# Level order, an earlier turn of K and half-array transposes in the RWKV recurrence of a two-block kernel

## The reference, cut to what matters

```python
def _rwkv7_step(S, inp):
    r, w, k, v, kk, a = inp
    sa = jnp.einsum('dbhij,dbhj->dbhi', S, -kk)
    S = S * w[..., None, :] + sa[..., None] * (kk * a)[..., None, :] + v[..., None] * k[..., None, :]
    y = jnp.einsum('dbhij,dbhj->dbhi', S, r)
    return S, y
```

## Time and profile before

| | us |
|---|---|
| median of three runs | 2919.23 |
| the profiled execution's own time | 2922.75 |
| its span | 2921.0 |
| TensorE busy in the span | 2863.0 |
| VectorE busy in the span | 1467.3 |
| ScalarE busy in the span | 1085.4 |

### The profile page before, as it was taken

The page is one execution under the profiler, slowest core; times in us unless marked ns, Lnnn a source line. Parts: engine busy times, 40 slices in busy tenths (PEclk is TensorE's granted clock), DMA queues, the critical chain, the costliest instruction groups (busy, mean ns, idle before and its releaser), DMA issues.

```text
span 2921.0 us, 43018 instructions
## 1 busy us (share of the span) xinstructions
PE 2863.0 (98%) x19334; PEld 2365.6 (81%) x19334; DVE 1467.3 (50%) x1431; ACT 1085.4 (37%) x1176; POOL 174.8 (6%) x94
## 2 busy tenths in 40 slices
PE   9999999999999999999999999999998998999998
PEld 7787788888889888888888888788877886888886
DVE  6766553443454544343454344555666555544432
ACT  5554532222454732222342223442244432332222
POOL 1002110000100010000110000330000000100001
PEclk9999999999999999999999999999999999999999
DMA  4220022323222022223222233321240003222222
GB/s 148 73 76 2 30 87 101 101 90 119 101 90 87 30 87 88 100 101 108 101 98 90 101 103 112 112 80 65 87 133 4 3 5 133 87 101 101 98 98 79
DMA packets 44887, 249.06 MB, mean 85 GB/s; under 512 B 8443, under 2 KB 12283, under 8 KB 17184
## 3 DMA queue, kind: packets, MB, share of 16 engines
q1 hardware_dynamic: 43552, 242.11, 24.2%
q10 hardware_dynamic: 1152, 4.19, 0.4%
HBM read 237.90 MB, written 8.39 MB: 84 GB/s over the span
## 4 chain that ended last, share of the span: by engine, by line
PE 91%; DVE 5%; ACT 3%; issue 1%; DMA 0%; POOL 0%; SPq 0%; DVEq 0%; ACTq 0%
PE ps L667 75%; PE ps L2909 6%; PE ps L1522 1%; PE ps L2493 1%; PE ps L2203 1%; PE ps L3961 1%; PE ps L2477 1%; PE ps L3944 1%; PE ps L3973 1%; PE ps L2174 0%; PE ps L3083 0%; DVE wlo L274 0%; DVE gdn_conv L1147 0%; ACT whi L268 0%; PE ps L426 0%
## 5 line engine op out<-in xcount | busy, mean ns | idle before, releaser
L274 DVE TENSOR_TENSOR wlo<-wraw,whi 128x2048 fp32r<-128x2048 f32 x210 | 486.5, 2317 | 911.0 <-ACT whi L268 906.9
L268 ACT ACTIVATE whi<-wraw 128x2048 fp32r<-128x2048 f32 x210 | 402.1, 1915 | 900.1 <-PE ps L667 900.1
L667 PE MATMUL ps<-ffn_xh,whi 128*128 128x512 f32 x1408 | 549.2, 390 | 0.2 <-DVE wlo L274 0.2
L667 PE MATMUL ps<-ffn_xh,wlo 128*128 128x512 f32 x1408 | 547.8, 389 | 0.0
L667 PE MATMUL ps<-ffn_xl,whi 128*128 128x512 f32 x1408 | 547.8, 389 | 0.0
L667 PEld LDWEIGHTS ps<-ffn_xh,whi 128*128 128x128 f32 x1408 | 264.3, 188 | 57.0 <-DVE wlo L274 1.0
L667 PEld LDWEIGHTS ps<-ffn_xl,whi 128*128 128x128 f32 x1408 | 264.3, 188 | 55.6 <-issue 0.7
L667 PEld LDWEIGHTS ps<-ffn_xh,wlo 128*128 128x128 f32 x1408 | 264.3, 188 | 54.7
L667 PE MATMUL ps<-ffn_uh,whi 128*128 128x512 f32 x704 | 274.1, 389 | 0.0
L667 PE MATMUL ps<-ffn_uh,wlo 128*128 128x512 f32 x704 | 273.9, 389 | 0.0
L667 PE MATMUL ps<-ffn_ul,whi 128*128 128x512 f32 x704 | 273.9, 389 | 0.0
(11 more groups left out here) (518 smaller groups left out, 4485.9 us busy)
## 6 DMA issues: line engine op xcount, KB each, us to landing
wraw<-in_weights SPq DMA_DIRECT2D x211, 1024.0 KB, 4.9
gates_kept<-gates_tmp ACTq DMA_DIRECT2D x8, 512.0 KB, 4.1
mix_gate<-gates_kept SPq DMA_DIRECT2D x8, 512.0 KB, 11.2
h<-in_x SPq DMA_DIRECT2D x4, 512.0 KB, 8.3
mix_y<-hz_kept SPq DMA_DIRECT2D x2, 1024.0 KB, 6.4
out<-out SPq DMA_DIRECT2D x4, 512.0 KB, 3.1
wraw<-in_weights SPq DMA_DIRECT2D x2, 512.0 KB, 6.7
ple_raw<-in_p SPq DMA_DIRECT2D x4, 256.0 KB, 5.2
```

The source lines that it names most:

```text
L268: c.nc.scalar.activation(c.whi[:, j % 2, :], c.wraw[:, j % 2, :], ACT.Copy).then_inc(c.hi_ready, 1)
L274: c.nc.vector.tensor_tensor(c.wlo[:, j % 2, :], c.wraw[:, j % 2, :], c.whi[:, j % 2, :].bitcast(F32), ALU.subtract).then_inc(c.lo_ready, 1)
L667: last = nc.tensor.matmul(pair[:, m, :], a, b, start=opens and n == 0 and wa + xa == 0, stop=closes and n == len(ks) - 1 and wa == 1)
```

## The change

Three edits. The level order becomes L L R R at every level: slots 7 to 25 hold L00 L01 R00 R01 L10 L11 R10 R11 and so on up to L40 L41 R40, then slot 26 the turn of `K`, slot 27 R41, slot 28 the turn of `B`. The turn of `K` goes to `A_BANK` and `C_BANK`, so it waits for the last `y` of the pair that steps, and the first z of the next steps waits for `Kt`. `pe_strict` now waits for the last `XT` of the build before, and the products with `Bt` wait for `Bt`. Third, in every turn the head on partitions 0 to 63 is turned by a transpose instruction in place of a matmul; the other head stays a matmul.

```diff
+    def turned(self, out, src):
+        nc, ident, (one, two) = self.c.nc, self.c.ident, self.halves()
+        nc.tensor.transpose(out(one), src(one), ident[one, one])
+        return nc.tensor.matmul(out(two), src(two), ident[two, two], start=True, stop=True)
...
         if part == 0:
+            if n == 0:
+                pe.wait_ge(*self.at("Kt", p))
             pe.wait_ge(*self.at("ST", 8 * p + n))
...
-                if n == 0:
-                    pe.wait_ge(*self.at("Kt", p))
...
             if n < NCH - 1:
+                if n == 0:
+                    pe.wait_ge(*self.at("Bt", p))
...
-        elif s in (7, 8):
-            self.pe_left(pe, k, 0, s - 7)
-        elif s == 9:
-            self.pe_right(pe, k, 0, 0)
-        elif 10 <= s < 26:
-            l, what = 1 + (s - 10) // 4, (s - 10) % 4
-            if what in (0, 2):
-                self.pe_left(pe, k, l, what // 2)
+        elif 7 <= s < 26:
+            l, what = divmod(s - 7, 4)
+            if what < 2:
+                self.pe_left(pe, k, l, what)
             else:
-                self.pe_right(pe, k, l - 1 if what == 1 else l, int(what == 1))
+                self.pe_right(pe, k, l, what - 2)
         elif s == 26:
+            pe.wait_ge(*(self.at("y", 8 * k - 1) if k else self.shift.free(len(RW_ORDER) - 1)))
+            self.pe_turn(pe, self.K[k % 2], (self.A_BANK, self.C_BANK), "tK")
+        elif s == 27:
             self.pe_right(pe, k, LEVELS - 1, 1)
-        elif s == 27:
-            self.pe_turn(pe, k, self.B, self.Z_BANK, "tB")
         elif s == 28:
-            self.pe_turn(pe, k, self.K, self.F_BANK, "tK")
+            pe.wait_ge(*self.at("XT", 10 * k + 2 * (LEVELS - 1)))
+            self.pe_turn(pe, self.B[k % 2], self.Z_BANK, "tB")
...
         elif k:
-            pe.wait_ge(*self.at("Kt", k - 1))
+            pe.wait_ge(*self.at("XT", 10 * k - 1))
```

More of the change, by code:

```diff
@@ L2750, in __init__ @@
         self.sems = {}
-        for engine, cycles in (("pe", ("kk", "lora", "vt", "BA", "KA", "MV", "Y", "Z", "tB tK", "z", "U", "dS",
+        for engine, cycles in (("pe", ("kk", "lora", "vt", "BA", "KA", "MV", "Y", "Z", "tK tB", "z", "U", "dS",
                                        "bonus turn g")),
                                ("act", ("u12", "kk2 log rs", "se sl s", "eB eR fac", "t3", "vtc", "XTe", "LT", "MVc", "ysc", "Yc",
[1 row of a table removed]
[1 row of a table added]
                                ("dve", ("neg", "eye", "floor nkk", "scan b kdir B K R A", "kd bonus1",
@@ L2845, in sync @@
             self.load_pair(sp, p, self.gl, self.gl_loaded, 2)
-        sp.wait_ge(*self.at("tK", HP - 1))
+        sp.wait_ge(*self.at("tB", HP - 1))
         sp.wait_ge(*self.at("dS", 8 * HP - 9))
@@ L3051, in pe_right, with pe_turn @@
         last.then_inc(*self.done("Z"))
-    def pe_turn(self, pe, k, what, banks, name):
-        src = what[k % 2]
-        pe.wait_ge(*self.at("XT", 10 * k + 2 * (LEVELS - 1) + (banks is self.F_BANK)))
+    def pe_turn(self, pe, src, banks, name):
         for d in range(2):
             for n in range(NCH):
-                last = self.both(lambda r: self.bank(banks[d])[r, n, :], lambda r: src[r, d, n, :],
-                                 lambda r: self.c.ident[r, r])
+                last = self.turned(lambda r: self.bank(banks[d])[r, n, :], lambda r: src[r, d, n, :])
         last.then_inc(*self.done(name))
@@ L3088, in pe_prepare @@
             for n in range(NCH):
-                last = self.both(lambda r: out[r, n, :], lambda r: u[r, 2 * HP + p, n * C7:(n + 1) * C7],
-                                 lambda r: self.c.ident[r, r])
+                last = self.turned(lambda r: out[r, n, :], lambda r: u[r, 2 * HP + p, n * C7:(n + 1) * C7])
             last.then_inc(*self.done("vt"))
@@ L3102, in pe_finish @@
             for n in range(NCH):
-                last = self.both(lambda r: out[r, n, :], lambda r: self.yp[r, n, :], lambda r: self.c.ident[r, r])
+                last = self.turned(lambda r: out[r, n, :], lambda r: self.yp[r, n, :])
             last.then_inc(*self.done("turn"))
@@ L3166, in act_build @@
                     .then_inc(*self.done("ysc"))
[L3167 to L3172, removed]
+        if 7 <= s < 26 and (s - 7) % 4 < 2:
+            self.act_left(act, k, *divmod(s - 7, 4))
+        elif s in (26, 28):
+            name, dst, banks = (("tK", self.Kt, (self.A_BANK, self.C_BANK)), ("tB", self.Bt, self.Z_BANK))[(s - 26) // 2]
             act.wait_ge(*self.at(name, k))
@@ L3347, in dve_build @@
                 .then_inc(*self.done("ys"))
[L3348 to L3353, removed]
+        if 7 <= s < 26 and (s - 7) % 4 >= 2:
+            l, what = divmod(s - 7, 4)
+            self.dve_right(dve, k, l, what - 2)
+        elif s == 27:
             self.dve_right(dve, k, LEVELS - 1, 1)
@@ L3410, in dve_prepare @@
             if p >= 2:
-                dve.wait_ge(*self.at("tK", p - 2))
+                dve.wait_ge(*self.at("tB", p - 2))
             eB = self.eB[:, :, 1 - d:1 - d + C7]
```

## The result

The changed kernel takes 3011.66 us (median of four runs, 3010.88 to 3014.51), the kernel before 2919.27 (2918.84 to 2923.47): the ratio is 1.0315 [1.0297, 1.0333], 3.2% slower, where 2912.3 was forecast and 2920.5 was the end of the range. The profiled execution took 3011.53 us, its span 3009.7.

A forecast was written before the change was run, and what follows sets the result against it. TensorE, busy for 98% of the span, was taken as the bound, so only its lost time in the recurrence could be won: 3.4 (level order) + 3.5 (early `K`) + 0 (transposes) = 6.9 us less, 2912.3; range 2905 to 2920.5.

The forecast's parts named there:

- One head by transposes: In the turns' 192 chunks: quarters keep their own pace, so 0; bounds 5.6 us won, 11.2 lost.
- Rival 4: In the 192 chunks: a transpose holds the array for itself, up to 58 ns each, 2923.5 us; chance 0.14.
- The clock: In the recurrence: pauses of like sum remain, so no change; bounds 4.3 us won, 5.1 lost.
- K turned early: Before the next build's first product: the wait for `Kt` goes, 1.15 us in three periods, 3.5 us less.
- Level order: In the recurrence's levels: TensorE's waits for `X` go, partly replaced by waits for `ST` and `Zs`; 3.4 us less.
- Rival 1: In the recurrence: VectorE and ScalarE take the level order's whole gain, only `Kt` waits go, 2915.7 us; chance 0.20.
- Rival 2: In the turns: issue is the bound, so transposes win 5.6 us more, 2906.7 us; chance 0.12.
- Rival 3: In period 1: the clock's fall goes with the pauses ahead of it, 4.3 us more won, 2908.0; chance 0.18.

The follow-up runs named there:

- e1: The changed kernel with both heads turned by plain matmuls again, level order and early turn of `K` kept: 2914.21 us, ratio 0.9981.
- e9: e1 with the first head's product in the large turns a plain matmul 128 columns wide, no transposes: 3022.96 us, ratio 1.0355.
- e3: The kernel before with the early turn of `K` alone, old level order and plain turns: 2916.61 us, ratio 0.9993.
- e4: The changed kernel with all transposes of a turn first, then all its matmuls: 2931.99 us, ratio 1.0043.
- e2: The kernel before with the level order L L R R alone, `K` turned last, plain turns: 2918.20 us, ratio 0.9997.
- e8: e1 with VectorE's preparation of the next pair one slot later, and period 0's late taps and `ST` reset moved: 2906.76 us, ratio 0.9958.
- e5: The changed kernel with transposes and matmuls of a turn alternating in groups of four chunks: 2954.80 us, ratio 1.0121.

## Why the prediction was wrong, by its steps

- **One head by transposes: this step failed.** It was priced at nothing, "each quarter has its own pace", with 11.2 us as the upper bound. The runs show 59 us in the turns at full clock, and, through the clock, about 40 more (21 in the turns, 15 to 19 outside); e1 puts the whole at 97. Two things were wrong in it. First, show four transposes in a row and one quarter alone, never a transpose between quarters, and their pace was taken for the pace of the mixture. The first of those four stands 149 ns behind the quarter's last record, so the price was in these rows too, at their edge. Second, the bound only counted the transposes' own 58 ns; a bound has to hold the cost of going from one kind of instruction to the other. That was in the trace of before, in the recurrence itself:

```profile
2254.26 2.03 PE L2909 MATMUL ps<-rw_vt,rw_MQ 64*64 64x64 f32 x64
2256.23 1.12 PE L3083 MATMUL ps<-rw_u,rw_wa 64*128 64x512 f32 x2
2257.28 0.45 PE L2909 MATMUL ps<-rw_Zs,rw_XT 64*64 64x64 f32 x8
```

  64 records usually take 1.87 to 1.89 us; ahead of the wider L3083 they take 1.97. Record by record, the last one of the quarters starts 149 ns ahead of L3083's first, where otherwise a pair of them comes every 58 ns. With a change each way at every chunk, 384 x 0.13 = 50 us, the forecast would have been above 2960 even with no clock in it. The Trainium skill says it too (TensorEngine Tiling (Array Packing), Key Properties): changing the tiling mode, not merely the tile, drains the engine. It gives no price; here it is 0.148 us into the wider shape and 0.17 to 0.20 us back. The prediction had weighed another line of that page and missed this one.
- **Rival 4** had the right place and sign, and the first part of its price: a transpose does hold the array for itself, 192 x 56 ns = 10.8 us against the 11.2 worked out. It lacked the price of each change, more than four times as much. It had a chance of 0.14, and its time, 2923.5, stood outside the range.
- **The clock** was put at nothing, 4.3 won to 5.1 lost. After, it was down for 122.9 us of the recurrence. The bound counted pauses between groups of the new order; what a turn of 48 records does once it is broken up by changes wasn't asked, since the step above had none. The busy share doesn't warn of it either: in the 10 us ahead of 2328.5, still at full clock, PE is busy for 10.00, and for 20.50 of 20.50 in the stretch at 1.2 GHz; the modelled ends of the matmuls cover the 0.15 us between starts. That transposes aren't needed for it is shown by e9, which has none in the large turns, nor elsewhere in the recurrence, and 136.5 us at the lower clock. How the chip comes to lower it there stays open. And the 4.3 on the winning side couldn't be won: it was measured in the profiled execution, while the median from which it was taken is that of runs without such a fall (the mean clock was 0.999 in 18 of 27).
- **K turned early** was right in kind: no wait for `Kt`, z directly ahead of the strict product. Its size was 3.5; e3 shows 2.5. The term left out R41's copy, which now ends so late that z waits for the reset of `ST`, 0.3 to 0.4 us in three periods of four; "period 4: nothing won or lost" is one of them.
- **Level order** was right by its waits: `X` from 8.2 us to 2.5 in e1, `ST` from 4.6 to 6.9. With early `K` it gives 6.7 at equal clock, against 6.9 forecast. That near hit is partly luck: at equal clock e3 is 2.4 below (nine runs of 2916.51 in the median), which leaves 4.3 to the level order, so one term was 1.1 too large and the other 0.9 too small. In the medians the two give 4.9, since only one of e1's 11 runs had a mean clock of 0.999; that loss is inside the bound "5.1 lost".
- **Rival 1** (only the `Kt` waits go) would have been 2915.7; e1's median lies 1.5 below it, its best run 3.5. **Rival 2** (issue) is out: no turn became shorter, and in e4 one quarter alone keeps 58 ns a record. **Rival 3** (the clock's fall goes) is out as well: in the new order the clock falls more often (e1, e2). In e8's five runs no long fall came, but its gain doesn't hang on that. And the rival's 2908.0 took 4.3 us off a median that held no such fall.

## What to carry to other kernels

Price an instruction by its neighbours, not by rows of its own kind in a row: where an edit alternates two shapes on TensorE's array, look for the one place in the trace where the shapes already meet, measure from the last start to the first, and multiply by the number of changes. If it must be done, group it (e4: 2.90 us a turn in place of 6.85, though still 17.8 us slower in all than plain turns). Both heads by transposes, with no change inside a turn, was not run; at e4's pace a large turn would be an estimated 32 x 56 ns = 1.8 us, hardly less than a plain one's 1.87. And look at the clock after every edit of TensorE's order: what a better order wins can be lost to a fall of the clock, as in most runs of e2. Then look for the pauses that remain: shortening them gave e8 6.5 us and more over e1 at equal clock.

## What the runs showed of the hardware

- At full clock a change from a 64x64 quarter to a wider shape (64x128, 72x128, 128x128) takes 148 to 151 ns from start to start, to a transpose and to a plain matmul alike, and 199 behind a product with 128 moving columns. Back it is 171 to 175 ns after a lone 64x64 transpose, 145 after a row of them (e4, e5) and 202 after the wide matmul of e9. At 1.2 GHz a chunk with two changes takes 0.65 us against 0.43.
- A fp32 transpose of a 64x64 block takes 56 ns in a row of its kind, but doesn't overlap with matmuls of the other quarter. Between a transpose and a plain matmul that both fill the array there is no such price: 109 ns, the pace of the row.
- The two records of a lone quarter matmul are 107 ns apart when they stand between two changes (0.16 us at 1.2 GHz); in a row the records of one quarter come every 58.
- The granted clock was at 1.2 GHz in stretches of up to 37.5 us in which TensorE was busy for 94 to 100% by the records, and it fell to it from 10 us with a busy share of 100% (at 2328.5). A microsecond at the lower clock cost 0.34 to 0.42 us here.
